# Norms in halves of 512 tokens, next stage's first chunks multiplied before they are scaled: a 1-core block of two layers and an mLSTM/S5 layer

## The reference, cut to what matters

```
def rmsnorm(x, g):
    y = xf * lax.rsqrt(jnp.mean(xf * xf, axis=-1, keepdims=True) + RMS_EPS)
    return (y * g.astype(jnp.float32)).astype(x.dtype)

for layer in range(2):
    h = rmsnorm(x, mix_pre_g[layer])
    m = even_mixer(h, ...) if layer % 2 == 0 else odd_mixer(h, ...)
    x = x + rmsnorm(m, mix_post_g[layer])
    h = rmsnorm(x, ffn_pre_g[layer])
    x = x + rmsnorm((silu(h @ w_gate) * (h @ w_up)) @ w_down, ffn_post_g[layer])
# then one layer with two branches side by side
xn = rmsnorm_2(x, norm_pre_g)
proj = xn @ w_in            # 7176 columns: mLSTM, S5 and the gates
x = x + rmsnorm_2((g_a * (mlstm @ w_a_out) + g_b * (s5 @ w_b_out)) @ w_o, norm_post_g)
```

## Time and profile before

| | |
|---|---|
| median of 3 runs | 3796.38 us (3792.73 to 3797.72) |
| profiled execution | 3794.27 us |
| its span in the trace | 3791.4 us |
| mean granted TensorE clock | 0.957 of full |
| TensorE busy | 91% |
| VectorE, GpSimd, ScalarE busy | 47%, 41%, 19% |

### The profile page before, as it was taken

The page is one execution under the profiler, slowest core; times in us unless marked ns, Lnnn a source line. Parts: engine busy times, 40 slices in busy tenths (PEclk is TensorE's granted clock), DMA queues, the critical chain, the costliest instruction groups (busy, mean ns, idle before and its releaser), DMA issues. The chain is left out here.

```text
span 3791.4 us, 40722 instructions
## 1 busy us (share of the span) xinstructions
PE 3459.4 (91%) x15904; PEld 2800.8 (74%) x15904; DVE 1776.6 (47%) x1746; ACT 731.2 (19%) x923; POOL 1540.6 (41%) x720
## 2 busy tenths in 40 slices
PE   6999898999999979986999999989787999989897
PEld 4777686888888867765888888868666777767685
DVE  4444425332332367675323323259665566565542
ACT  3333312000000033333100000021111223122110
POOL 4111645433443463445434433466642422413255
PEclk9999899999999999997999999989889999999998
DMA  3110022111111221121111111123212210101122
GB/s 102 40 29 26 17 84 73 51 50 50 50 44 50 89 73 39 44 89 56 51 50 50 44 50 44 50 106 89 65 52 78 87 35 28 53 22 53 33 78 105
DMA packets 246568, 215.78 MB, mean 57 GB/s; under 512 B 7988, under 2 KB 213428, under 8 KB 246472
## 3 DMA queue, kind: packets, MB, share of 16 engines
q1 hardware_dynamic: 225888, 165.14, 14.7%
q10 hardware_dynamic: 20584, 49.31, 3.7%
HBM read 180.78 MB, written 29.43 MB: 55 GB/s over the span
## 5 line engine op out<-in xcount | busy, mean ns | idle before, releaser
L331 POOL TENSOR_TENSOR w_hi<-raw,one_col 128x1024 fp32r<-128x1024 f32 x265 | 528.2, 1993 | 1921.2 <-PE ps L345 1866.2
L343 PE MATMUL ps<-H_hi,w_hi 128*128 128x512 f32 x2848 | 1138.7, 400 | 89.1 <-DVE H_lo L529 23.6
L345 PE MATMUL ps<-H_hi,w_lo 128*128 128x512 f32 x2848 | 1119.4, 393 | 0.0
L344 PE MATMUL ps<-H_lo,w_hi 128*128 128x512 f32 x2848 | 1119.0, 393 | 0.0
L343 PEld LDWEIGHTS ps<-H_hi,w_hi 128*128 128x128 f32 x2848 | 541.5, 190 | 218.5 <-issue 49.5
L333 POOL TENSOR_TENSOR w_lo<-raw,w_hi 128x1024 fp32r<-128x1024 f32 x265 | 667.0, 2517 | 20.7
L345 PEld LDWEIGHTS ps<-H_hi,w_lo 128*128 128x128 f32 x2848 | 540.8, 190 | 115.0
L344 PEld LDWEIGHTS ps<-H_lo,w_hi 128*128 128x128 f32 x2848 | 541.9, 190 | 109.0 <-issue 1.9
L1037 DVE TENSOR_TENSOR Y<-Y,ps 128x1024 f32<-128x1024 f32 x176 | 213.0, 1218 | 183.0 <-PE ps L345 183.0
L343 PE MATMUL ps<-ffn_f_hi,w_hi 128*128 128x512 f32 x704 | 273.9, 389 | 0.0
L344 PE MATMUL ps<-ffn_f_lo,w_hi 128*128 128x512 f32 x704 | 273.9, 389 | 0.0
(11 more groups left out here) (443 smaller groups left out, 4628.0 us busy)
## 6 DMA issues: line engine op xcount, KB each, us to landing
raw<-in_w_in SPq DMA_DIRECT2D x49, 512.0 KB
raw<-in_ffn_w_gate SPq DMA_DIRECT2D x44, 512.0 KB
raw<-in_ffn_w_up SPq DMA_DIRECT2D x44, 512.0 KB
raw<-in_ffn_w_down SPq DMA_DIRECT2D x44, 512.0 KB
x_dram<-b_X ACTq DMA_DIRECT2D x32, 512.0 KB, 2.6
b_X<-x_dram SPq DMA_DIRECT2D x4, 4096.0 KB, 13.7
raw<-in_ev_w_in SPq DMA_DIRECT2D x17, 512.0 KB
b_X<-in_x_t SPq DMA_DIRECT2D x2, 4096.0 KB, 13.3
```

The lines of the kernel that those rows point to most:

```text
L331: pool.tensor_tensor(w_hi[s][:, :n], raw[s][:, :n], one_col[:, :].broadcast_to([P, n]), ALU.mult).then_inc(split_hi, 1)
L343: pe.matmul(o, l_hi, r_hi, start=first, stop=False)
L344: pe.matmul(o, l_hi, r_lo, start=False, stop=False)
L345: return pe.matmul(o, l_lo, r_hi, start=False, stop=last)
```

## The change

The boundary works by halves of 512 tokens. Of each half X is loaded, the first norm's r copied by ScalarE from PSUM to SBUF (`copy`), then tile by tile VectorE makes the new x in Y (`x_new`), ScalarE H_hi = gain·x without r, VectorE H_lo, and TensorE multiplies the first three chunks of the next stage by it (`part`). The fourth chunk follows when r_pre is there (`last_chunk`). Before the two FFNs H stays without r, and `dve_block` multiplies gate and up by r_pre as they leave PSUM. Before attention, LRU and S5 (`normalize`) VectorE scales the three products in PSUM (`scale_parts`) and makes H anew with r (`h_fill`, `h_low`). GpSimd adds nothing to X or H any more. A fourth slot, in the temporaries, serves the FFNs' and the LRU's first phase; the tuples of 4 and 5 chunks change. The constants are made in the first FFN, behind its block 0.

```diff
-    slots, out = {3: (0, 1, 2), 2: (0, 1), 4: (0, 1, 2, 1), 5: (0, 1, 2, 0, 1), 6: (0, 1, 2) * 2,
+    slots, out = {3: (0, 1, 2), 2: (0, 1), 4: (0, 1, 2, 0), 5: (0, 1, 2, 3, 0), 6: (0, 1, 2) * 2,
                   7: (0, 1, 2, 0, 1, 2, 1), 10: (0, 1, 2) * 3 + (1,), 12: (0, 1, 2) * 4}, []
     for name, count, body in listed:
+        if name in ("ffn0_first", "ffn1_first"):
+            out.append((name, count, body, (0, 1, 2, 3)))
+            continue
...
+    w_hi.append(nc.alloc_sbuf_tensor_at("w_hi3", [P, 1024], F32R, offset=tmp_at + TMP_BYTES - 3 * S * 4))
+    w_lo.append(nc.alloc_sbuf_tensor_at("w_lo3", [P, 1024], F32R, offset=tmp_at + TMP_BYTES - 2 * S * 4))
...
+        X = nc.alloc_sbuf_tensor_at(f"{tag}_X", [P, KT, S], F32, offset=h_hi_at if x_at is None else x_at) if post else Y
+        t2, t3, r_post, r_pre = carve(*[(f"{tag}_{n}", [P, S], F32) for n in ("t2", "t3", "r_post", "r_pre")], keep=R_AT - 3 * S * 4)
+        sq0, sq1, y_sum, spreads, roots, inverses = carve(
+            *[(f"{tag}_{n}", [P, S], F32) for n in ("sq0", "sq1", "y_sum")], (f"{tag}_spreads", [KT, 4, P], F32),
+            (f"{tag}_roots", [KT, 2, P], F32), (f"{tag}_inverses", [KT, 2, P], F32), keep=stat_at)
...
+            def copy(stat, h):
+                wait(e, "spread", number(stat, h))
+                e.activation((r_pre if stat else r_post)[:, halves[h]], ps[:, 6 + h if stat else h, :], ACT.Copy).then_inc(q["rows"], 1)
...
+            def raw(h, k):
+                i = KT * h + k
+                if post:
+                    wait(e, *x_made(h, k))
+                elif k == 0:
+                    wait(e, f"x_loaded{h}", 16)
+                e.activation(H_hi[:, k, halves[h]], Y[:, k, halves[h]], ACT.Copy, scale=col(pre, k)).then_inc(q["raw"], 1)
+                if i >= 4:
+                    wait(e, "summed", (i - 4) // 2 + 1)
+                e.activation(squares[i % 4], Y[:, k, halves[h]], ACT.Square).then_inc(q["raw"], 1)
+                if post:
+                    e.dma_start(x_dram_t[:, k, halves[h]], Y[:, k, halves[h]]).then_inc(q["x_stored"], 16)
...
+            def part(h):
+                for k in range(KT):
+                    wait(e, "raw_low", KT * h + k + 1)
+                    for c in range(3):
+                        if h == 0 and k == 0:
+                            e.wait_ge(split, stream.number(seam[0], seam[1] + c))
+                        ins = step(h, c, k)
+                        if k == KT - 1:
+                            ins.then_inc(q["part_done"] if normalize or h == 0 else multiplied, 1)
+                    if h and k == 1:
+                        x_add(0, 3)
+                    if h and k == 5:
+                        spread(1, 0)
+                    if k in (3, 5, 7):
+                        x_add(h, k // 2 - 1)
+
+            def last_chunk(h):
+                wait(e, *copied(1, h))
+                if h == 0:
+                    e.wait_ge(split, stream.number(seam[0], seam[1] + 3))
+                for k in range(KT):
+                    if normalize:
+                        wait(e, *h_split(h, k))
+                    ins = step(h, 3, k)
+                if h:
+                    ins.then_inc(multiplied, 1)
...
+            if seam:
+                split_chunks(e, seam[0], seam[1], seam[1] + 4)
...
+            def x_new(h, k):
+                i = KT * h + k
+                if k == 0:
+                    wait(e, *copied(0, h))
+                    wait(e, f"x_loaded{h}", 16)
+                if i >= 4:
+                    wait(e, "x_made", 2 * (i - 4) + 2)
+                e.scalar_tensor_tensor(scaled_to[i % 4], Y[:, k, halves[h]], col(post, k), r_post[:, halves[h]], ALU.mult, ALU.mult).then_inc(q["x_made"], 1)
+                wait(e, "x_made", 2 * i + 1)
+                e.tensor_tensor(Y[:, k, halves[h]], X[:, k, halves[h]], scaled_to[i % 4], ALU.add).then_inc(q["x_made"], 1)
+
+            def raw_low(h, k):
+                i = KT * h + k
+                wait(e, "raw", 2 * i + 1)
+                e.scalar_tensor_tensor(H_lo[:, k, halves[h]], Y[:, k, halves[h]], col(pre, k), f32(H_hi[:, k, halves[h]]), ALU.mult, ALU.subtract).then_inc(q["raw_low"], 1)
+
+            def pair_up(h, i):
+                wait(e, *squared(h, 2 * i + 1))
+                e.tensor_tensor(squares[2 * i % 4], squares[2 * i % 4], squares[2 * i % 4 + 1], ALU.add).then_inc(q["paired"], 1)
+
+            def raw_half(h):
+                for k in range(KT):
+                    if post:
+                        x_new(h, k)
+                    if k:
+                        raw_low(h, k - 1)
+                    if h and k == 4:
+                        inverse(1, 0)
+                    if k in (3, 5, 7):
+                        pair_up(h, k // 2 - 1)
+                raw_low(h, KT - 1)
+                pair_up(h, 3)
+
+            def scale_parts(h):
+                wait(e, *copied(1, h))
+                for c in range(3):
+                    wait(e, "part_done", 3 * h + c + 1)
+                    ins = e.tensor_tensor(ps[:, 2 * c + h, :], ps[:, 2 * c + h, :], r_pre[:, halves[h]], ALU.mult)
+                    if h:
+                        ins.then_inc(multiplied, 1)
+            def h_fill(h, k):
+                i = KT * h + k
+                if i >= 2:
+                    wait(e, *h_split((i - 2) // KT, (i - 2) % KT))
+                e.scalar_tensor_tensor(full_to[k % 2], Y[:, k, halves[h]], col(pre, k), r_pre[:, halves[h]], ALU.mult, ALU.mult).then_inc(q["h_dve"], 1)
+
+            def h_low(h, k):
+                wait(e, "h_hi", KT * h + k + 1)
+                e.tensor_tensor(H_lo[:, k, halves[h]], full_to[k % 2], f32(H_hi[:, k, halves[h]]), ALU.subtract).then_inc(q["h_dve"], 1)
...
+                raw_half(0)
+                raw_half(1)
+                if normalize:
+                    for h in range(2):
+                        scale_parts(h)
+                        for k in range(KT):
+                            h_fill(h, k)
+                            if k:
+                                h_low(h, k - 1)
+                            if h == 0 and k == 4:
+                                inverse(1, 1)
...
+        done = [(q[n], b[n] + totals[n]) for n in (("x_made", "x_stored") if post else ()) + (("raw", "raw_low", "summed", "rows") if pre else ())
+                + (("h_dve",) if n_norm else ())]
...
+                e.wait_ge(multiplied, stream.number(name, at + 2 * t, i))
+                e.wait_ge(*f_ready(b - 1, t))
+                e.tensor_tensor(a[t][:, :], pair(2 * t), r_pre[:, :], ALU.mult).then_inc(f_dve, 1)
                 e.wait_ge(tanh_done, 2 * b + t + 1)
-                e.scalar_tensor_tensor(a[t][:, :], th[t][:, :], 1.0, pair(2 * t), ALU.add, ALU.mult).then_inc(gated, 1)
-                e.wait_ge(gated, 2 * b + t + 3)
+                e.scalar_tensor_tensor(a[t][:, :], th[t][:, :], 1.0, a[t][:, :], ALU.add, ALU.mult).then_inc(f_dve, 1)
                 e.wait_ge(multiplied, stream.number(name, at + 2 * t + 1, i))
-                e.scalar_tensor_tensor(f[t][:, :], a[t][:, :], 0.5, pair(2 * t + 1), ALU.mult, ALU.mult).then_inc(f_full, 1)
+                e.scalar_tensor_tensor(up[t][:, :], pair(2 * t + 1), 0.5, r_pre[:, :], ALU.mult, ALU.mult).then_inc(f_dve, 1)
+                e.wait_ge(*up_scaled(b, t))
+                e.tensor_tensor(a[t][:, :], a[t][:, :], up[t][:, :], ALU.mult).then_inc(f_dve, 1)
                 e.wait_ge(f_hi_done, 2 * b + t + 1)
-                e.tensor_tensor(f_lo[par_][:, t, :], f[t][:, :], f32(f_hi[par_][:, t, :]), ALU.subtract).then_inc(f_ready, 1)
+                e.tensor_tensor(f_lo[par_][:, t, :], a[t][:, :], f32(f_hi[par_][:, t, :]), ALU.subtract).then_inc(f_dve, 1)
...
             dve_steps(e)(e.memset(Y[:, :, :], 0.0))
             dve_block(e, B, 0, first, 0, 0)
+            if l == 0:
+                pl["dve"](e)
...
-            split_chunks(e, first, SLOTS)
+            split_chunks(e, first, 4)
...
-            pe_in(e, 0, first, 0, ready=h_ready)
...
-            gemm("u0", ready=h_ready)
-            gemm("u1")
-            gemm("gt", after("u0"))
-            gemm("g0", after("u1"))
-            turns(0, 0, "gt")
+            turns(0, 0, "u0")
...
+    b0 = boundary("b0", None, "mix_pre0", A["x_t"], None, [], [], ("fox", 0))
+    fx = fox(b0["tmp_free"])
+    b1 = boundary("b1", "mix_post0", "ffn_pre0", A["x_t"], fx["y_ready"], fx["x_free"], fx["sq_free"], ("ffn0_first", 0), x_at=tmp_at, normalize=False)
+    f0 = ffn(0, b1["tmp_free"], b1["r_pre"])
+    b2 = boundary("b2", "ffn_post0", "mix_pre1", x_dram, f0["y_ready"], f0["x_free"], f0["sq_free"], ("lru_first", 0))
+    lr = lru(b2["tmp_free"])
+    b3 = boundary("b3", "mix_post1", "ffn_pre1", x_dram, lr["y_ready"], lr["x_free"], lr["sq_free"], ("ffn1_first", 0), normalize=False)
+    f1 = ffn(1, b3["tmp_free"], b3["r_pre"])
+    b4 = boundary("b4", "ffn_post1", "norm_pre", x_dram, f1["y_ready"], f1["x_free"], f1["sq_free"], ("s5", 0))
```

## The result

The changed kernel takes 3908.22 us (median of 4 runs, 3905.62 to 3909.63) against 3797.05 for the kernel before (4 runs of the same comparison): a ratio of 1.0294, 95% interval 1.0276 to 1.0312. It is slower by 111 us where I forecast 60, outside the range. The profiled execution took 3908.06, its span is 3906.3, 114.9 more than before.

The account below looks back on a forecast made before the run. TensorE was taken as the bound, busy 3459.4 of 3791.4 us. Terms +15 −14.9 +9 +18.2 +1.5 −10.5 +26.0 +18.0 −1.9 = +60.4 on 3794.27 gave 3854.7, then 3856 with the median 2.1 higher; range 3815 to 3888.

Parts of the forecast that it names:

- The constants: FFN 0: small operations between VectorE's blocks 0 and 1 make TensorE wait, +9 us (5 to 12).
- The entry of the LRU: Normalised boundary before LRU: entry 88.6 us after TensorE's last product before the boundary, previously 56.2, +32.4; net +18.2.
- my 14.2 for waits that are gone: LRU: 14.2 us of the 42.9 from entry to the gate's tanh were waits for products that now stand ready.
- The raw half: Each boundary's 16 half tiles: VectorE needs 2.22 us each, 35.5, plus reciprocal 0.9 and tails 1.3, 37.7 in all.
- the turns: Boundaries, merge and output: VectorE and GpSimd wait out each other's SBUF instructions, 51.6 us of the sum.
- Seams 1 and 3: Boundaries before FFN 0 and FFN 1, without normalising: block 1 starts earlier, −14.9 and −10.5 us.
- Merge and output: Shared slot makes TensorE wait for a split in four passes: 3.0 + 5.3 + 5.3 + 4.4 = +18.0 us.
- S5's seam: Normalised boundary before S5: entry 84.3 us after TensorE's last product before it, previously 54.65, +29.7; net +26.0.
- Attention's stretch: Start of the program through attention: first filler at 120 us against 104.45, +15.
- rival 1: Turn-taking of VectorE and GpSimd costs half, 25.8 us gone: 3827 (3812 to 3838), chance 0.15.
- Rivals 2 and 3: No turn-taking: 3801, chance 0.05; late LRU, S5 and attention entries hidden behind TensorE's four chunks: 3788, chance 0.08.
- Rival 4: TensorE's clock halved in the boundaries: nine matmuls take 4.1 against VectorE's 2.22, up to 30 us each; 3890 and more, chance 0.07.

Follow-up runs that it names:

- e8_two: Changed kernel with the third of three early chunks multiplied by only one of its eight tiles (wrong product): span 3889.5 us against 3906.3.
- e4_lo: Changed kernel with GpSimd's w_lo made for only 16 of 1024 columns in the first three chunks of four boundaries: span 3885.9 us against 3906.3.
- e7_both: Changed kernel with e4_lo's edit and six of eight second-norm sums per boundary cut from four matmuls to one: span 3882.1 us against 3906.3.
- e5_consts: Changed kernel with the constants back at the start instead of in the first FFN: span 3915.6 us against 3906.3.
- e1_slots: Changed kernel with slot tuples (0, 1, 2, 1) and (0, 1, 2, 3, 1), last chunk never sharing the next pass's first slot: span 3888.4 us against 3906.3.
- h1_ffn: Kernel before with the new boundary only ahead of both FFNs, the new FFN, and Y cleared behind block 0: span 3790.9 us against 3791.4.
- h2_acc: h1_ffn with each half's squares added up on VectorE and one TensorE sum per half instead of four: span 3784.2 us against 3790.9.
- h3_tanh: h2_acc with ScalarE's tanh table loaded ahead of the FFN's entry wait: span 3773.1 us, 11.1 less than h2_acc.

## Why the prediction was wrong

**What held.** The direction and its chief reason: VectorE and GpSimd take turns, and the late entries of attention, LRU and S5 lengthen these stages. The entry of the LRU came 39.3 us later after E than before (the clearing at 1468.17, in the kernel before at 1397.40), where I had 32.4. Less my 14.2 for waits that are gone this gives +25.1; the stretch grew by 27.2. FFN blocks in their steady state cost nothing: TensorE's products come 31.5 us later than before in FFN 0 and 62.0 in FFN 1, the same from block 2 to the last. The end gained 1.0 (I had 1.9).

**The step that failed** is "The raw half": "times 16 = 35.5, plus a reciprocal of 0.9 and 1.3 of tails: 37.7", and the 2.5 behind it. I priced the raw half by VectorE's instructions alone (4.4 for a pair of half tiles), without a wait, and held TensorE to have room. Without the turns, VectorE's raw half took 47.1, 46.8, 45.3 and 46.5 us in seams 1 to 4. Of these it stood idle for 9.4, 9.1, 7.5 and 8.7, above all for ScalarE's H_hi; what is left is 37.6 to 37.8, so the instructions were priced rightly and the waits were put at nothing. The queues behind this are TensorE's and ScalarE's. TensorE has 18 matmuls of 0.228 for a pair and a sum that costs 1.30 from product to product: 5.4. ScalarE can't square before TensorE's sum frees a buffer, nor copy r_pre before TensorE's spread, and H_hi stands behind both. From the first early product to the last it took 46.7 to 48.1 us in all four seams, however late it began. TensorE was idle for only 2.0 to 2.6 of these, and 20, 18, 7 and 16 of the 144 matmuls ran at the lower clock, 0.2 longer each; the rest, 42 to 43 us in every seam, is TensorE's own queue at the upper clock.

By my numbers the last early product was due at E + 53.1, 59.8, 59.8 and 55.5; it came at 64.0, 69.3, 65.8 and 64.7, which is 35.6 us later in all. Not all of this reached the end, as making H anew took less than I had: block 1 of the FFNs came later by more than it, but the LRU's entry was 7.0 late and S5's 4.0. So it accounts for at most 27.9 (10.9 + 7.0 + 6.0 + 4.0) of the 54.5 that I was short; attention's entry was 4.7 late as well, and e8_two, with fewer products on TensorE, took 5.8 off it. What the experiments show: e8_two, that taking products off TensorE takes 5.7 to 6.8 us off in three of four seams, and that the ring then holds the pace, so that easing TensorE's queue alone gains no more; e4_lo and e7_both, that the turns hardly change the length. Not tested is another place for the spread and the copy of r_pre: the reciprocal for it was ready 7.0 us before TensorE spread it in all four seams; VectorE then waits 3.4, TensorE 1.11, and in three of four seams 7 or 8 products at the lower clock follow. That 16 half tiles make the sum dearer (more, smaller sums) was in the diff; I didn't add up TensorE's queue.

**Other terms.** Seams 1 and 3 have 1.9 more between the copy of r_pre and the clearing (seam 3: 1880.15 and 1882.01), and seam 3 has 2.9 because TensorE starts block 1 at the lower clock after 10.45 us of idling (the block's four chunks took 46.4 us instead of 43.5; in seam 1, behind the same idling, 45.2); I had neither. Seam 3 was 11.0 late at block 1: 6.0 by the last early product, 3.0 because r_pre stood in SBUF 9.4 behind it where I had 6.4 (TensorE's spread stands behind half of the fourth chunk), and the 1.9. With the 2.9 this is the 13.8 by which the stretch missed. The turns in seam 3 cost 9.6 (six operations from 1813.05 to 1826.78 instead of some 4.1) where I had 12.1. Over all seams VectorE's prolonged boundary operations lasted 33.4 us beyond 0.72 each, where I had 51.6, so that some 18 too much here hid a part of what the raw half was short of; e4_lo puts twelve low parts at 20.4. I had also written that the boundary's operations weren't prolonged before: those that read r from PSUM (L515, L535) never took over 1.28, but L529, with two SBUF inputs, took 3.12 once in each of seams 1, 2 and 4. The constants cost 7.9 (e5_consts) where I had 9. Merge and output cost 26.4 where I had 18.0: the four passes set TensorE back by 3.8, 7.7, 7.7 and 7.2 against the kernel before; the waits for w_lo are 4.5 to 5.5, with 10 to 12 matmuls at the lower clock behind each (I had 3.0, 5.3, 5.3 and 4.4, without these); in the first the kernel before waited too. e1_slots gives 23.4 back. The LRU's slots cost nothing where I had 1.5. S5's seam cost 27.5 where I had 26. Attention's stretch cost 21.7 where I had 15.

**The rivals.** Half-priced turns (rival 1, 25.8 of 51.6) were nearer than the full price for the turns (33.4), but the time came out on the other side, as what they spared was lost to the raw half's pace. Rivals 2 and 3 didn't come. Rival 4 had the right place, a half tile's nine matmuls against VectorE's 2.22, and its reason in small: the pitch was 0.43 for the first 7 to 12 matmuls of the four seams and for 7 or 8 late ones in three, 1.4 to 4.0 us a seam instead of up to 30. At 0.23 the nine matmuls (2.05) do fit behind 2.22; with their share of the sum (0.65) they don't.

## What to carry to other kernels

When work is overlapped, add up the queue of each engine of the overlapped stretch for one step of it, small sums and the gaps around them included; the slowest queue sets the pace, not the one that was alone before. Then follow the ring of waits through all engines for one step: it can be as long as the slowest queue, and then relieving that queue gives only a part. An early product buys nothing if what follows it waits for a later point than before: look for the entry waits, the clearing and the table loads that were hidden behind TensorE's work and now end the chain. A slot table read as the smallest distance over all passes lets one shared slot at the seam of two passes put a wait in every pass.

## What the runs showed of the hardware

TensorE's sum of four 128x128 fp32 matmuls between two products costs 1.30 us of its queue (0.32 to its start, 0.97 to the next product), whereas products follow each other at 0.228. A table load taken out of ScalarE's path saved more than twice its 1.28 us on TensorE's wait (3.20 to 0.45), as VectorE's instruction then came ahead of GpSimd's instead of into it (1.22 against 2.73): with turns, a small shift decides who waits.

TensorE's clock is at one of two levels, and the idle time before a matmul alone doesn't tell which. In seam 1 of the changed kernel the first dozen early products had a pitch of 0.43, at a granted clock of 0.50, the level of 1.2 GHz; 0.23 is the pitch at 1.00, 2.4 GHz (windows of the early products; columns as above):

```profile
core 0: us, PE busy (x) PEld busy (x) DVE busy (x) ACT busy (x) POOL busy (x), PEclk, DMA share, GB/s
613.50:618.50 5.00, 4.97 (x12) 3.96 (x13) 4.93 (x8) 3.08 (x6) 0.00 (x0) 0.50 0.69 240
619.00:640.00 21.00, 20.26 (x97) 14.91 (x97) 16.23 (x25) 8.08 (x13) 0.00 (x0) 1.00 0.20 76
```

After 10.45 us of idling in seam 3 (changed kernel) the first matmul took 0.79. After 3.20 it took 0.79 in h1_ffn and 0.49 in h2_acc, where the matmuls grew to 0.62 only 0.8 us later; after 0.45 (h3_tanh) it took 0.49. At the copy of r_pre TensorE idles for 1.11 in all four seams. In seam 4 the first matmul behind it takes 0.79, in seams 1 and 2 the matmuls grow to 0.6 within 0.7 us, and in seam 3 they stay at 0.4. TensorE's timeline in seam 1:

```profile
655.80 0.50 PE L350 MATMUL ps<-H_hi,w_hi 128*128 128x512 f32 x1 [1.11 <-DVE H_lo L607]
...
656.79 0.63 PE L350 MATMUL ps<-H_hi,w_hi 128*128 128x512 f32 x1
```
